# GpSimd makes low parts of the shifted norms, sums of squares in three parts, key selection spread anew

## The reference, cut to what matters

```python
def rms_norm(x, g):
    y = xf * lax.rsqrt(jnp.mean(xf * xf, axis=-1, keepdims=True) + EPS)
    return (y * g.astype(jnp.float32)).astype(x.dtype)

def modulate(h, shift, scale):
    return h * (1.0 + scale) + shift

x = x + 0.5 * swiglu(rmsnorm(x, g_ffn1[l]), w1_gate[l], w1_up[l], w1_down[l])
...
score = jnp.where(causal[None], score, -jnp.inf)
_, sel = lax.top_k(score, top_k)
...
x = x + 0.5 * ml[2] * swiglu_2(modulate(rms_norm(x, norm1_g[layer]), ml[0], ml[1]), ...)
```

## Time and profile before

| | |
|---|---|
| median of 3 runs | 2587.27 us (2586.76 to 2588.53) |
| profiled execution | 2586.84 us, span 2585.1 us, granted PE clock 0.999 |
| PE busy | 2542.6 us, 98% |
| DVE, ACT, POOL busy | 1348.1 us (52%), 749.7 us (29%), 380.9 us (15%) |
| chain that ended last | PE 93%, DVE 4%, ACT 1%, issue 1% |

### The profile page before, as it was taken

How to read it: one execution, slowest core, us unless ns; L and a number is a source line. 1 busy time by engine, 2 the same in 40 slices (tenths; PEclk the granted TensorE clock), 3 DMA queues, 4 the chain that set the end, 5 groups by cost and what they waited for, 6 DMA issues and landing times.

```text
span 2585.1 us, 33121 instructions
## 1 busy us (share of the span) xinstructions
PE 2542.6 (98%) x12274; PEld 2076.1 (80%) x12274; DVE 1348.1 (52%) x1968; ACT 749.7 (29%) x1031; POOL 380.9 (15%) x317
## 2 busy tenths in 40 slices
PE   8999999989999999999999999999999999999998
PEld 6888888755788888788888888888888778888887
DVE  7666657789476433454444443544227653433333
ACT  3222233368432222411111111323322552222223
POOL 1101023020120111311011011103001004111112
PEclk9999999999999999999999999999999999999999
DMA  6444434221244332333333321233321012333331
GB/s 185 149 134 149 141 104 107 50 65 33 87 133 136 96 98 81 102 98 98 98 98 97 98 84 63 73 91 98 97 91 33 17 66 82 95 99 84 98 93 69
DMA packets 365920, 243.57 MB, mean 94 GB/s; under 512 B 21504, under 2 KB 363648, under 8 KB 365824
## 3 DMA queue, kind: packets, MB, share of 16 engines
q1 hardware_dynamic: 365824, 242.28, 32.1%
HBM read 237.79 MB, written 2.10 MB: 93 GB/s over the span
## 4 chain that ended last, share of the span: by engine, by line
PE 93%; DVE 4%; ACT 1%; issue 1%; POOL 0%; DMA 0%; DVEq 0%; SPq 0%; ACTq 0%; POOLq 0%
PE PS L947 24%; PE PS L954 24%; PE PS L949 24%; PE PS L922 4%; PE PS L925 4%; PE PS L923 4%; PE PS L1505 2%; PE PS L1290 1%; PE PS L1497 1%; DVE VA L1939 1%; PE PS L877 1%; PE PS L1257 1%; PE PS L1122 0%; PE PS L1455 0%; PE PS L1457 0%
## 5 line engine op out<-in xcount | busy, mean ns | idle before, releaser
L947 PE MATMUL PS<-NH,WH 128*128 128x512 f32 (+1 forms) x2112 | 615.3, 373 | 4.2 <-DVE WL L1918 1.9
L949 PE MATMUL PS<-NH,WL 128*128 128x512 f32 (+1 forms) x2112 | 613.0, 371 | 0.0
L954 PE MATMUL PS<-NL,WH 128*128 128x512 f32 (+1 forms) x2112 | 584.9, 372 | 0.0
L1918 DVE TENSOR_TENSOR WL<-RAW,WH 128x2048 fp32r<-128x2048 f32 (+1 forms) x187 | 465.1, 2487 | 101.4 <-ACT WH L1535 99.4
L1535 ACT ACTIVATE WH<-RAW 128x2048 fp32r<-128x2048 f32 (+2 forms) x188 | 357.5, 1902 | 499.5 <-PE PS L954 493.4
L954 PEld LDWEIGHTS PS<-NL,WH 128*128 128x128 f32 x2112 | 385.2, 188 | 71.3 <-POOL NL L2612 0.7
L949 PEld LDWEIGHTS PS<-NH,WL 128*128 128x128 f32 x2112 | 384.7, 188 | 70.7
L947 PEld LDWEIGHTS PS<-NH,WH 128*128 128x128 f32 x2112 | 382.0, 188 | 73.6 <-issue 6.1
L2570 POOL CAST HH<-VA 128x512 f32 (+2 forms) x88 | 60.9, 692 | 1300.6 <-DVE VA L2079 1300.6
L1609 ACT ACTIVATE SA<-PS 128x512 f32<-128x512 f32 x104 | 62.2, 598 | 628.9 <-PE PS L954 595.6
L947 PE MATMUL PS<-HH,WH 128*128 128x512 f32 (+1 forms) x820 | 238.1, 371 | 0.0
(11 more groups left out here) (370 smaller groups left out, 2580.0 us busy)
## 6 DMA issues: line engine op xcount, KB each, us to landing
RAW<-in_ffn_w_in SPq DMA_DIRECT2D x88, 512.0 KB, 4.9
MW<-in_w_mod SPq DMA_DIRECT2D x72, 512.0 KB, 3.5
RAW<-in_w_in SPq DMA_DIRECT2D x70, 512.0 KB, 4.1
RAW<-in_w_gate SPq DMA_DIRECT2D x44, 512.0 KB, 4.0
RAW<-in_w_up SPq DMA_DIRECT2D x44, 512.0 KB, 5.2
RAW<-in_w_down SPq DMA_DIRECT2D x32, 512.0 KB, 4.0
RAW<-in_ffn_w_out SPq DMA_DIRECT2D x32, 512.0 KB, 4.1
RAW<-in_w_out SPq DMA_DIRECT2D x16, 512.0 KB, 3.9
```

Source lines behind the costliest of these rows:

```text
L947: pe.matmul(outs[half][x], w[half][0], xh(k), start=i == 0, stop=False)
L949: pe.matmul(outs[half][x], w[half][1], xh(k), start=False, stop=False)
L954: last = pe.matmul(outs[half][x], w[half][0], xl(k), start=False, stop=i == kn - 1)
L1918: dve.tensor_tensor(WL[1 - s][:, 0:cols], RAW[1 - s][:, 0:cols], WH[1 - s][:, 0:cols].bitcast(F32), ALU.subtract).then_inc(w_lo, 1)
```

## The change

Three things. (1) `pooled` is now (3, 5, 7) also for norms with a shift, so that POOL makes three of the eight low parts of norm_x1, norm_x2 and norm_x3. DVE added the shift in the operation that made the low part; POOL first adds it in place (TENSOR_SCALAR), waits for that, and subtracts. (2) POOL adds the squares of tiles 1 to 5 only; PE makes twelve matmuls with ones, for the running sum, tile 6 and tile 7. (3) The steps of the choice of keys stand elsewhere: three fewer in stage 9, two more in the index loop, none between the first key copies and the attention's loop (three before), and four more at units 7 and 8.

```diff
-        norm_lo2 = sem("norm_lo2")
+        norm_lo2, norm_sh = sem("norm_lo2"), sem("norm_sh")
...
-                self.early, self.sums = early, 0 if rows else 2 if early else n
-                self.pooled = (3, 5, 7) if dst and not shift and n == KD else ()
+                self.early, self.sums = early, 0 if rows else 3 if early else n
+                self.pooled = (3, 5, 7) if dst and tok == T and n == KD else ()
...
-                sums = (0, m.n - 1) if m.early else range(m.n) if part is None else (part,)
+                sums = (0, m.n - 2, m.n - 1) if m.early else range(m.n) if part is None else (part,)
...
-                        pe.wait_ge(norm_acc, m.acc + m.n - 2)
+                        pe.wait_ge(norm_acc, m.acc + m.n - 3)
...
                 if n == 9:
                     norm_inverse(norm_q)
-                    selected(4)
+                    selected(3)
...
-                    selected(3 if n == 8 else 2)
+                    selected(3 if n == 8 else 0)
...
-                if N1 + 9 <= n < N1 + 16:
+                if N1 + 7 <= n < N1 + 16:
                     selected(1)
...
             keys_copied(0, 1)
-            selected(3)
...
+                elif u + AHEAD == 10:
+                    selected(3)
                 elif u + AHEAD == 11:
+                    selected(1)
                     rope_cos(1)
                     keys_copied(1, 0)
...
+            dve.wait_ge(*low_ready(norm_x2, KD - 2))
             dve.wait_ge(*low_ready(norm_x2, KD - 1))
...
             def norm(m):
-                for k in range(1, m.n - 1):
+                for k in range(1, m.n - 2):
...
                 for k in m.pooled:
                     pool.wait_ge(norm_hi, m.low + k + 1)
                     h, l = m.dst(k)
+                    if m.shift:
+                        pool.tensor_scalar(scaled(m, k), scaled(m, k), m.shift(k), None, ALU.add).then_inc(norm_sh, 1)
+                        pool.wait_ge(norm_sh, len(m.pooled) * SHIFTED.index(m) + m.pooled.index(k) + 1)
                     pool.tensor_tensor(l, scaled(m, k), h.bitcast(F32), ALU.subtract).then_inc(norm_lo2, 1)
...
             norm(norm_x1)
-            final_sum(KD - 2)
-            final_sum(KD - 1)
+            for k in range(KD - 3, KD):
+                final_sum(k)
+            lows(norm_x1)
...
             norm(norm_x2)
+            lows(norm_x2)
...
             norm(norm_x3)
+            lows(norm_x3)
```

More of the change, by code:

```diff
@@ L339, in __init__ @@
                 self.applied = True
-                self.early, self.sums = early, 0 if rows else 2 if early else n
-                self.pooled = (3, 5, 7) if dst and not shift and n == KD else ()
+                self.early, self.sums = early, 0 if rows else 3 if early else n
+                self.pooled = (3, 5, 7) if dst and tok == T and n == KD else ()
                 self.lo, self.lo2 = sum(m.n - len(m.pooled) for m in norms if m.dst), sum(len(m.pooled) for m in norms)
-                self.mm, self.acc = sum(m.sums for m in norms), sum(m.n - 2 for m in norms if m.early)
+                self.mm, self.acc = sum(m.sums for m in norms), sum(m.n - 3 for m in norms if m.early)
                 self.low = sum(m.n for m in norms if m.dst)
@@ L617, in build @@
         norm_x3 = modulated(4, x_src, T, n_dst, pairs_ready(wo2_b), True)
+        SHIFTED = [norm_x1, norm_x2, norm_x3]
         norm_out = Norm(x_src, KD, T, lambda k: vec("final", k), None, ready=stream_ready(ffn4), early=True)
```

## The result

| | before | changed |
|---|---|---|
| median of 10 runs | 2586.87 us (2586.19 to 2588.53) | 2593.68 us (2591.07 to 2594.53) |
| ratio | | 1.0023, 95% interval 1.0015 to 1.0032 |
| profiled execution | 2586.84 us, span 2585.1 | 2591.07 us, span 2589.3 |

A forecast was written before the change was run, and what follows sets the result against it. TensorE was taken as the bound, busy 2542.6 of 2585.1 us. Low parts +2.1, sums +0.7 and moved keys -1.9 gave +0.9 on 2586.84; with 0.43 from profile to median, 2588.2 us, range 2585.2 to 2591.0.

The forecast's parts named there:

- the term of the low parts: Low parts 3, 5, 7 on POOL: norm_x1 0, norm_x2 +1.0, norm_x3 +1.1; +2.1 us in all.
- stage 9: Projection stage with three key-selection steps removed: PE's wait for the latent key norm's split ends 1.30 us sooner.
- the attention start: Three steps and a threshold pass go; DVE 2.75 us sooner, of which 2.5 stays because ACT must end its query copies.
- the sums of norm_x1: Sums of squares in three parts: -0.84 us in norm_x1, where PE's wait for POOL's sixth add goes.
- norm_x1's low parts: Low parts 3, 5, 7 of norm_x1 on POOL: cost 0, covered by PE's longer parts.
- the moved keys: Key-selection steps moved between stage 9, index loop, attention start and units 7 and 8: -1.9 us, bounds -3.3 to 0.
- the fourth step: Last of four steps returned at units 7 and 8, ahead of the key copies: 0.6 us, wholly on the path.
- The collision: In norm_x3, DVE's split and POOL's part 7 exclude each other: split 2.2 us, subtraction ending 1.16 behind it.
- my own sign: POOL's subtraction for part 7 of norm_x3 should take over 2.5 us; the forecast is wrong if it takes 1.3.
- Rival 1: DVE and POOL don't collide as in norm2: low parts -0.65 instead of 2.1, total 2585.5 us; chance 0.14.
- rival 3: The moved key steps bring nothing, since DVE, ACT and PE are nearly full early in the attention: 2590.1 us; chance 0.15.
- Rival 4: Reload ahead of POOL's first TENSOR_SCALAR in norm_x1: up to 6.6 us lost, 2594.8; chance 0.12 for any loss.

The follow-up runs named there:

- e7: Kernel before with only low part 5 of each shifted norm on GpSimd, its add in three forms, one per norm; one profiled execution, no median given.
- e3: Kernel before with only the change's low parts on GpSimd, a one-input copy replacing the add of the shift; 2589.72 us, ratio 1.0008.
- e1: Kernel before with only the change's low parts 3, 5, 7 on GpSimd, keys and sums as before; 2597.51 us, ratio 1.0038.
- e13: Kernel before with only 7 filler products on PE ahead of its wait for the latent key norm; 2586.79 us, ratio 0.9995.
- e12: Kernel before with only the change's low parts on GpSimd, the shift added by a two-input TENSOR_TENSOR; 2592.76 us, ratio 1.0019.
- e9: Kernel before with moved keys, norm_x1's third sum block, part 5 of norm_x2 and norm_x3 on GpSimd, 14 products before the latent key norm's wait; 2584.82 us.
- e11: Kernel before with moved keys, third sum block in norm_x1 alone, 7 products before the latent key norm's wait; 2582.55 us, ratio 0.9980.
- e4: The changed kernel run again, unaltered, against the kernel before; 2593.96 us, ratio 1.0022.
- e10: Changed kernel with filler products sized to fit within PE's waits in norm_x2 and norm_x3; 2592.77 us, ratio 1.0018.

## Why the prediction was wrong

**The step that failed** is the price of POOL's add of the shift, in the term of the low parts: "Bounds for the add: the one-input cast of 0.61 and the two-input subtraction of 1.29; it reads one tensor, so I take 0.61." It takes 1.57, above both ends. I had ordered the rows by how many tensors an operation reads; it is another operation than either, and e7 shows that it is dearer than a two-input one. A bound must come from the same operation or be called none.

**How it got large.** "2.07 for each part" became 3.1 to 3.5, and I counted it once, at part 7. But the high parts for POOL come 2.0 and 2.7 us apart when nothing holds them up (in norm_x3 of e3 they end at 2211.60, 2213.58 and 2216.29), and PE takes two parts in 2.7 us. At 3.1 POOL falls behind with each of the three, PE waits in three places, and the scale of tile 6 waits too, which puts the high part of 7 off. At 2.07 POOL doesn't fall behind and PE's wait for part 3 is only 0.23, which is why reckoning part 7 alone gave nearly the right answer for e3. The term of the low parts was +2.1 (bounds -0.65 to +3.4) and is +7.3.

**The clock** was no term at all. The profile of before had it at 1.00 up to its last matmul, and I took that for the kernel's nature. It was a rare execution: of the 81 executions of the kernel before that were timed with e1 to e13 only 7 have its mean granted clock, 0.999; 37 have 0.998 and 37 have 0.997, and these last take 1.7 us more in the mean than the 7. Of the nine profiles of e1 to e12 in which the wait at 531 stood unfilled, eight show it at half there (all but e7), for 1.2 to 1.4 us. In e7, and in e9 and e11, whose wait was filled, it fell at 18 to 22 us instead; so that the products kept it up at 531 isn't shown. Behind norm_x2 or norm_x3 it fell in two of the three profiles with TENSOR_SCALAR and bare waits (twice in e1, once in e4, 1.5 us each).

The trace of the change has +5.1 without a fall and the medians are +6.8 and +6.1 (e4). A fall is of the right size for the rest, but the recorded clocks don't bear it out: in the 20 executions of the changed kernel they average 0.9980, in those 81 of the kernel before 0.9976, so the changed kernel loses no more clock than the other; and e10's average, 0.9981, is no higher than the changed kernel's, nor is its gain resolved. What the 1.0 to 1.7 us between trace and medians are stays open. That PE's stop brings the falls in the norms is argued from this: each stands behind a stop of about 2 us, and in the two profiles with the stops filled there is none. But the first profile of the change and that of e12 have such stops without a fall, so this is thin evidence.

**The step from profile to median** was off as well: I added 0.43 from three runs, where ten give 0.03.

**Right, and for the reasons given:** stage 9 (-1.30); the attention start, where ACT's exponential begins at 552.18, right behind the query copies (552.16), as worked out; the wait at the key swap (0.97 for "near 0.9"); the sums of norm_x1 (-0.84), norm_x2 (+0.89) and norm_out (+0.42 for 0.45); norm_x1's low parts (+0.03). **Right with a wrong size:** the moved keys, -2.7 for -1.9: the attention start gave 0.4 more, and of the fourth step's 0.6 us only 0.2 came through: PE's wait at the swap grew by 0.65, its other waits on the way went from six to five and from 2.70 to 2.58 us, and the other 0.3 isn't placed. **The collision** in norm_x3 came, but on another operation than I told: the add of part 7 took 3.60, the subtraction behind it 1.26. By the letter of my own sign ("wrong if that one takes 1.3") that already spoke against the forecast.

**The rivals.** Rival 1 (no collision) and rival 3 (the moved steps bring nothing) are excluded by these rows. Rival 4 named nearly the measured time, by a cause that isn't there: the load stands at 1083.1, and POOL's first add begins at 1088.34, 0.10 us behind the end of its high part (1087.51 + 0.73), and has no other wait. So whatever the load starts was done within 5.2 us, under a wait that was there anyway.

```profile
L2617 POOLq MODIFY_POOL_CONFIG  x2: 9/9/9, 1083.1 to 1083.1; - x2
```
```profile
1088.34 1.57 POOL L2617 TENSOR_SCALAR VA<-VA,MOD 128x512 f32<-128x512 f32 x1 [5.20 <-ACT NH L1572]
```

The range was too short at its upper end, first because both bounds of the add rested on unlike rows, and then because the low parts' bounds were worked out one part deep.

## What to carry to other kernels

Where one engine feeds another in a chain, work out two numbers before anything is moved: the date by which the consumer wants each item after its input is there (here 2.0 us), and the pace at which items come (here 2.7 us); here a helper that kept the second and nearly the first (e3) cost 0.8 us a norm, and one that kept neither (the change) 3.6. An operation that no row shows has no upper bound in the rows of its neighbours: measure it first, alone, at a place with slack. And a stop of PE can cost more than its length, which one profile may not show: look at several.

## What the runs showed of the hardware

- POOL on 128x512 in float32, from SBUF to SBUF, where nothing delayed it: COPY 0.61 us, TENSOR_TENSOR with a repeated second input 1.04, TENSOR_TENSOR with two full inputs 1.29 to 1.31, TENSOR_SCALAR 1.50 with a number and 1.57 with a column of SBUF. The Trainium skill, GPSIMD Engine Reference, 4.1 Engine selection, has one-input operations roughly at line rate, and two-input ones as the slow ones; the trace agrees for the copy, and contradicts it for TENSOR_SCALAR.
- DVE's split of two SBUF inputs and a POOL operation shut each other out, also where POOL's reads a single tile: the add of 1.57 took 3.60 and ended 1.44 behind the split. That a DVE operation with two SBUF inputs contends with any GpSimd operation that reads SBUF is what the Trainium skill says too (SBUF — State Buffer, Who interferes with whom).
- PE's granted clock fell to 0.50 behind stops of 1.7 to 2.1 us between matmuls, in some executions of the same program and not in others, and that cost 1.2 to 1.6 us each time. It also fell where the last stops were shorter: at 560 in e13 (0.69 and 0.65, behind one of 2.11 at 555), and at 18 to 22 us in e7, e9 and e11 (up to 1.43).
- A wait of PE cost 0.2 to 0.3 us more than its row says: in norm_x2 of the change three new or longer waits make 2.85 us more, and the stretch grew by 3.62, the rest in the gap ahead of the wait's start and in the first products behind it (0.73 for two instead of 0.62).
